# The gated delta rule's output, its projection and the norms: work by halves, fused ops by quarters

## The reference

```python
def layer_norm(x, g, b):
    mu = jnp.mean(x, -1, keepdims=True)
    var = jnp.mean(jnp.square(x - mu), -1, keepdims=True)
    return (x - mu) * lax.rsqrt(var + LN_EPS) * g + b

# the end of gdn_mixer
o = gated_delta_rule_chunked(q, k, v, g, beta)      # 4 chunks of 64 tokens, 8 heads of 128
o = o * lax.rsqrt(jnp.mean(o * o, -1, keepdims=True) + NORM_EPS) * norm_g
o = o * jax.nn.silu(z)
return o.reshape(bsz, seq, GDN_V) @ w_out
```

## Time and profile before

| what | us |
|---|---|
| median of 3 runs | 1741.26 |
| lowest and highest of the runs | 1740.02, 1744.06 |
| the profiled execution's own time | 1741.66 |
| its span in the profile | 1739.9 |
| PE busy | 1518.2 (87% of the span) |
| DVE busy | 1059.4 (61%) |
| ACT busy | 660.8 (38%) |
| mean DMA rate over the span | 254 GB/s read from HBM |

### The profile page before, as it was taken

The page is one execution under the profiler, slowest core; times in us unless marked ns, Lnnn a source line. Parts: engine busy times, 40 slices in busy tenths (PEclk is TensorE's granted clock), DMA queues, the critical chain, the costliest instruction groups (busy, mean ns, idle before and its releaser), DMA issues.

```text
span 1739.9 us, 23377 instructions
## 1 busy us (share of the span) xinstructions
PE 1518.2 (87%) x9936; PEld 1132.8 (65%) x9936; DVE 1059.4 (61%) x1522; ACT 660.8 (38%) x834; POOL 4.9 (0%) x6
## 2 busy tenths in 40 slices
PE   7987977999967678999999998598899999998976
PEld 7976846889956566888888886486444434443324
DVE  6646646999769857888989887765222221222145
ACT  5562104444421237676767774241211101110113
POOL 0010000000000000000000000000000000000000
PEclk9998988999978798999999999698899999999998
DMA  8440013453531054998989898166699999999970
GB/s 348 143 151 3 2 49 128 168 232 146 204 147 51 1 194 154 345 352 336 350 318 352 337 349 321 52 239 259 275 428 427 428 427 427 428 428 429 428 314 24
DMA packets 36685, 443.37 MB, mean 255 GB/s; under 512 B 5344, under 2 KB 5728, under 8 KB 9184
## 3 DMA queue, kind: packets, MB, share of 16 engines
q1 hardware_dynamic: 34992, 437.03, 63.1%
q10 hardware_dynamic: 1584, 4.77, 0.7%
HBM read 440.74 MB, written 1.05 MB: 254 GB/s over the span
## 4 chain that ended last, share of the span: by engine, by line
PE 52%; DVE 10%; DMA 8%; ACT 1%; issue 1%; DVEq 0%; PEld 0%; ACTq 0%; PEldq 0%
PE psum L223 50%; DMA sb_spare<-moe_up 2%; DMA sb_work<-moe_up 2%; DMA sb_ring<-moe_up 2%; DVE sb_work L1404 1%; DVE sb_work L1405 1%; DMA sb_ring<-moe_wide 1%; DVE sb_small L298 1%; DVE sb_work L2284 1%; DVE sb_split L1674 1%; PE psum L1727 1%; DMA sb_lnp<-pT 0%; PE psum L2154 0%; PE psum L339 0%; DVE sb_ring_r L268 0%
## 5 line engine op out<-in xcount | busy, mean ns | idle before, releaser
L223 PE MATMUL psum<-sb_work 64*64 64x64 f32 (+9 forms) x3056 | 304.7, 371 | 51.0 <-DVE sb_work L1389 13.9
L1674 DVE TENSOR_TENSOR sb_split<-sb_ring,sb_split 128x2048 fp32r<-128x2048 f32 (+1 forms) x144 | 301.1, 2111 | 45.3 <-ACT sb_split L1668 44.6
L1668 ACT ACTIVATE sb_split<-sb_ring 128x2048 fp32r<-128x2048 f32 (+1 forms) x144 | 253.0, 1773 | 88.7 <-PE psum L223 52.3
L223 PEld LDWEIGHTS psum<-sb_work 128*64 128x64 f32 (+4 forms) x3056 | 165.1, 155 | 177.5 <-issue 135.5
L223 PE MATMUL psum<-sb_split 128*128 128x512 f32 (+1 forms) x912 | 268.9, 384 | 0.3 <-DVE sb_split L1943 0.3
L223 PE MATMUL psum<-sb_split,sb_lnp_r 128*128 128x512 f32 (+1 forms) x768 | 230.8, 374 | 2.3 <-DVE sb_split L1912 1.4
L223 PEld LDWEIGHTS psum<-sb_split 128*128 128x128 f32 x912 | 169.9, 188 | 30.6 <-DVE sb_split L1943 1.1
L223 PEld LDWEIGHTS psum<-sb_split,sb_lnp_r 128*128 128x128 f32 x768 | 142.8, 188 | 22.9 <-DVE sb_split L1912 1.6
L223 PE MATMUL psum<-sb_ring,sb_work 128*64 128x512 f32 (+1 forms) x576 | 142.3, 598 | 8.5 <-DVE sb_work L2284 4.7
L223 PE MATMUL psum<-sb_xT_r,sb_ring_r 128*128 128x256 f32 x512 | 147.6, 288 | 0.0
L2282 DVE TENSOR_TENSOR sb_work<-sb_work,psum 128x512 f32<-128x512 f32 x16 | 11.0, 689 | 171.4 <-ACT sb_work L2198 171.4
(11 more groups left out here) (405 smaller groups left out, 2557.5 us busy)
## 6 DMA issues: line engine op xcount, KB each, us to landing
sb_ring<-moe_wide SPq DMA_DIRECT2D x48, 2048.0 KB, 9.0
sb_work<-moe_up SPq DMA_DIRECT2D x33, 2048.0 KB, 23.8
sb_ring<-w_dense SPq DMA_DIRECT2D x24, 2048.0 KB, 9.1
sb_ring<-moe_up SPq DMA_DIRECT2D x20, 2048.0 KB, 26.8
sb_work<-moe_down SPq DMA_DIRECT2D x20, 2048.0 KB, 27.0
sb_ring<-moe_last SPq DMA_DIRECT2D x24, 1536.0 KB, 8.2
sb_ring<-ffn_wide SPq DMA_DIRECT2D x12, 2048.0 KB, 7.8
sb_ring<-moe_down SPq DMA_DIRECT2D x12, 2048.0 KB, 27.6
```

Of the source, the lines that this page charges most:

```text
L223: return nc.tensor.matmul(o, lhsT, rhs, start=start, stop=stop, **kw)
L1668: act.activation(wh[half_home(e, i)][:, 0:half_size(i)], half_raw(e, i), ACT.Copy).then_inc(sem("m1_high"), 1)
L1674: v.tensor_tensor(wl[home][:, 0:half_size(i)], half_raw(e, i), wh[home][:, 0:half_size(i)].bitcast(F32), ALU.subtract).then_inc(sem("m1_sp ...
```

## The change

The diff below is cut to what the stages run; left out are the counts of semaphores in later stages.

- `norm_half` is new. For n < 4 a half is normed in two quarters of 512 columns by two fused ops each: `(x - mean) * g`, then `(. * rstd) + b`. The wait for g and b stands ahead of the first, the wait for the root between the two pairs. Each quarter counts in `rows_normed`. For n = 7 one fused op of 1024 columns does both products. For n = 4 to 6 the op stays. All `rows_normed` counts are doubled.
- PE turns a half by quarters for n < 4 (`turn_half`), each as soon as it is normed. For n = 0 the banks are 0 to 3 instead of 4 to 7.
- The end of the GDN mixer goes by halves. ACT takes over the square, in four ops of 128x512, and the root is taken once for each half. DVE's reduce, small ops and reciprocal of half 0 (`inverted(0)`) stand ahead of chunk 3's ops, its gating (`gated(0)`) ahead of chunk 3's sum.
- PE transposes half 0 of `o`, does its first product, transposes half 1, and does the products in the order (half 0, columns 0), (0, 1), (1, 0), the turn of the normed half 0, (1, 1). DVE norms half 0 behind its second product.
- `released` for `w_out` waits for the third and the fourth product instead of the second and the fourth.
- Some semaphores of later stages are shared by two events that come one after the other: `logitsT_ps` with `logits_ps`, `gates_ready` with `mask_ready`, and those of the two expert stages' row splits. No instruction other than the counts changes there.

```diff
@@ -306,56 +306,80 @@
             dve_link(v, v.tensor_scalar(rtmp[:, h, :], mv[:, h, 1:2], eps, None, ALU.add))
             v.reciprocal(rtmp[:, h, :], rtmp[:, h, :]).then_inc(sem("var_inv"), 1)
 
+        def norm_half(v, n, y, xn, h):
+
+            if n < 4:
+                quarters = (slice(0, 512), slice(512, 1024))
+                if h == 0:
+                    v.wait_ge(sem("lnp_loaded"), 32 * (n + 1))
+                for f in quarters:
+                    ins = v.scalar_tensor_tensor(xn[:, h, f], y[:, h, f], mv[:, h, 0:1], lnp[:, 0, f], ALU.subtract, ALU.mult)
+                dve_link(v, ins)
+                v.wait_ge(sem("rstd_ready"), 2 * n + h + 1)
+                for f in quarters:
+                    v.scalar_tensor_tensor(xn[:, h, f], xn[:, h, f], rstd[:, h, :], lnp[:, 1, f], ALU.mult, ALU.add)\
+                     .then_inc(sem("rows_normed"), 1)
+                return
+            v.wait_ge(sem("rstd_ready"), 2 * n + h + 1)
+            if n < 7:
+                v.tensor_scalar(xn[:, h, :], y[:, h, :], rstd[:, h, :], None, ALU.mult).then_inc(sem("rows_normed"), 2)
+            else:
+                v.scalar_tensor_tensor(xn[:, h, :], y[:, h, :], rstd[:, h, :], lnp[:, 0, :], ALU.mult, ALU.mult)\
+                 .then_inc(sem("rows_normed"), 2)
+
         def norm_vector(v, n, y, xn):
 
             for h in range(HALVES):
-                v.wait_ge(sem("rstd_ready"), 2 * n + h + 1)
-                if n < 4:
-                    dve_link(v, v.tensor_scalar(xn[:, h, :], y[:, h, :], mv[:, h, 0:1], rstd[:, h, :],
-                                                ALU.subtract, ALU.mult))
-                    if h == 0:
-                        v.wait_ge(sem("lnp_loaded"), 32 * (n + 1))
-                    dve_link(v, v.tensor_tensor(xn[:, h, :], xn[:, h, :], lnp[:, 0, :], ALU.mult))
-                    v.tensor_tensor(xn[:, h, :], xn[:, h, :], lnp[:, 1, :], ALU.add).then_inc(sem("rows_normed"), 1)
-                elif n < 7:
-                    v.tensor_scalar(xn[:, h, :], y[:, h, :], rstd[:, h, :], None, ALU.mult).then_inc(sem("rows_normed"), 1)
-                else:
-                    dve_link(v, v.tensor_scalar(xn[:, h, :], y[:, h, :], rstd[:, h, :], None, ALU.mult))
-                    v.tensor_tensor(xn[:, h, :], xn[:, h, :], lnp[:, 0, :], ALU.mult).then_inc(sem("rows_normed"), 1)
-            v.wait_ge(sem("rows_normed"), 2 * n + 2)
+                norm_half(v, n, y, xn, h)
+            v.wait_ge(sem("rows_normed"), 4 * n + 4)
 
         def norm_scalar(act, n):
             for h in range(HALVES):
-                act.wait_ge(sem("var_inv"), 2 * n + h + 1)
-                act.activation(rstd[:, h, :], rtmp[:, h, :], ACT.Sqrt).then_inc(sem("rstd_ready"), 1)
+                norm_root(act, n, h)
+
+        def norm_root(act, n, h):
+            act.wait_ge(sem("var_inv"), 2 * n + h + 1)
+            act.activation(rstd[:, h, :], rtmp[:, h, :], ACT.Sqrt).then_inc(sem("rstd_ready"), 1)
+
+        def turn_bank(n, h, q):
+            return bank[2 * h + q if n == 0 else 4 + 2 * h + q]
+
+        def turn_half(pe, n, xn, h):
+
+            for q in range(2):
...
 
             t = TSTAGE[n]
             for h in range(HALVES):
-                pe.wait_ge(sem("rows_normed"), 2 * n + h + 1)
-                for q in range(2):
-                    for c in range(4):
-                        ins = pe.transpose(bank[4 + 2 * h + q][:, c * P:(c + 1) * P],
-                                           xn[:, h, (4 * q + c) * P:(4 * q + c + 1) * P], ident)
-                    ins.then_inc(sem("turned"), 1)
+                if n > 0 or h > 0:
+                    turn_half(pe, n, xn, h)
             pe.wait_ge(sem("xT_ready"), 4 * (t + 1))
             if n in (0, 1):
                 pe.wait_ge(sem("xl_ready"), 4 * (n + 1))
 
         def turn_evacuate(eng, n, gain, dst=None):
 
+            for h in range(HALVES):
+                turn_half_evacuate(eng, n, gain, dst, h)
+
+        def turn_half_evacuate(eng, n, gain, dst, h):
+
             t = TSTAGE[n]
-            for h in range(HALVES):
-                for q in range(2):
-                    eng.wait_ge(sem("turned"), 4 * t + 2 * h + q + 1)
-                    o = (xT if dst is None else dst)[:, 4 * q:4 * q + 4, h * P:(h + 1) * P]
-                    i = bank[4 + 2 * h + q][:, :].rearrange("p (c t) -> p c t", c=4)
-                    if gain is None:
-                        ins = eng.activation(o, i, ACT.Copy)
-                    else:
-                        ins = eng.tensor_tensor(o, i, bc(gain[:, 4 * q:4 * q + 4], 2, P), ALU.mult)
-                    ins.then_inc(sem("xT_ready"), 1)
+            for q in range(2):
+                eng.wait_ge(sem("turned"), 4 * t + 2 * h + q + 1)
+                o = (xT if dst is None else dst)[:, 4 * q:4 * q + 4, h * P:(h + 1) * P]
+                i = turn_bank(n, h, q)[:, :].rearrange("p (c t) -> p c t", c=4)
+                if gain is None:
+                    ins = eng.activation(o, i, ACT.Copy)
+                else:
...
@@ -639,21 +663,27 @@
                                 ins = mm(bank3(6 + b)[rr, i, :], DTo[rr, j, :], vnew[rr, j, :])
                         ins.then_inc(sem("oi_ps"), 1)
 
-            for G in range(NGRP):
-                h, h0 = G // 2, HD * (G % 2)
+            def turned_out(h):
                 pe.wait_ge(sem("o_gated"), h + 1)
-                for i in range(HD):
-                    ins = pe.transpose(bank[G][:, i * P:(i + 1) * P], o_rows[:, HD * G + i, :], ident)
-                ins.then_inc(sem("ot_ps"), 1)
-
-            pe.wait_ge(sem("ot_done"), NGRP)
-            for j in range(2):
+                for G in (2 * h, 2 * h + 1):
+                    for i in range(HD):
+                        ins = pe.transpose(bank[G][:, i * P:(i + 1) * P], o_rows[:, HD * G + i, :], ident)
+                    ins.then_inc(sem("ot_ps"), 1)
+
+            def projected(h, j):
                 unit_ready(pe, U_WOUT + j)
+                pe.wait_ge(sem("ot_done"), 2 * h + 2)
                 w = slot(U_WOUT + j).rearrange("p (k n) -> p k n", k=DC)
-                for h in range(HALVES):
-                    for k in range(DC):
-                        ins = mm(bank[4 + 2 * j + h][:, :], oT[:, k, h * P:(h + 1) * P], w[:, k, :], k == 0, k == DC - 1)
-                    ins.then_inc(sem("wout_ps"), 1)
+                for k in range(DC):
+                    ins = mm(bank[4 + 2 * j + h][:, :], oT[:, k, h * P:(h + 1) * P], w[:, k, :], k == 0, k == DC - 1)
+                ins.then_inc(sem("wout_ps"), 1)
+            turned_out(0)
+            projected(0, 0)
+            turned_out(1)
+            projected(0, 1)
+            projected(1, 0)
+            turn_half(pe, 0, xres, 0)
+            projected(1, 1)
 
         def gdn_scalar(act):
             act.dma_start(conv_w, I["conv_w"]).then_inc(sem("first_loaded"), 16)
@@ -720,14 +750,27 @@
             for G in range(NGRP):
                 act.wait_ge(sem("wt_ps"), G + 1)
                 act.activation(grp(wT, G).rearrange("p i (c t) -> p c i t", c=2), wt_ps(G), ACT.Copy).then_inc(sem("wt_done"), 1)
-            act.wait_ge(sem("oms_inv"), 1)
-            act.activation(of[:, :, :], of[:, :, :], ACT.Sqrt).then_inc(sem("gates_act"), 1)
-            for G in range(NGRP):
-                h, h0 = G // 2, HD * (G % 2)
-                act.wait_ge(sem("ot_ps"), G + 1)
-                act.activation(oT[:, h0:h0 + HD, h * P:(h + 1) * P], bank3(G), ACT.Copy).then_inc(sem("ot_done"), 1)
-            norm_scalar(act, 0)
-            turn_evacuate(act, 0, None, xT_r)
+            def squared(h):
+                for G in (2 * h, 2 * h + 1):
+                    act.wait_ge(sem("o_sum"), G + 1)
+                    act.activation(grp(Wm, G), grp(o_rows, G), ACT.Square).then_inc(sem("o_squared"), 1)
+
+            def rooted(h):
+                act.wait_ge(sem("oms_inv"), h + 1)
+                act.activation(of[:, h, :], of[:, h, :], ACT.Sqrt).then_inc(sem("gates_act"), 1)
+            squared(0)
+            rooted(0)
+            squared(1)
+            for h in range(HALVES):
+                for G in (2 * h, 2 * h + 1):
+                    act.wait_ge(sem("ot_ps"), G + 1)
+                    act.activation(oT[:, HD * (G % 2):HD * (G % 2) + HD, h * P:(h + 1) * P], bank3(G), ACT.Copy)\
+                       .then_inc(sem("ot_done"), 1)
+                if h == 0:
+                    rooted(1)
+            for h in range(HALVES):
+                norm_root(act, 0, h)
+                turn_half_evacuate(act, 0, None, xT_r, h)
 
         def gdn_vector(v):
...
@@ -848,6 +891,25 @@
 
             v.wait_ge(sem("uu_done"), NGRP)
             v.wait_ge(sem("t_done"), 5 * NGRP)
+
+            def inverted(h):
+                v.wait_ge(sem("o_squared"), 2 * h + 2)
+                m, o, r = oms[:, h, :], of[:, h, :], rq_s[:, h, :]
+                dve_link(v, v.tensor_reduce(m, Wm[:, HEADS * h:HEADS * (h + 1), :], AX.X, ALU.add))
```

(46 more changed lines are left out.)

63 lines of the change are left out of this document (26 added, 37 removed).

## The result

The kernel with the change takes **1727.35 us** (median of four runs, 1726.48 to 1728.09) against 1741.9 for the kernel before in the same comparison (1740.02 to 1744.06): a ratio of 0.9917, 95% interval 0.9902 to 0.9932. Faster by 0.8%, inside the range of 1721 to 1731, and 1.95 us above the forecast of 1725.4. The profiled execution took 1727.54, its span is 1725.8 where it was 1739.9.

What follows compares the result with a forecast made beforehand. PE was taken to wait in short stretches while DVE works alone. Terms 5.8 + 4.5 + 1.1 + 2.0 + 1.35 + 1.5 = 16.25 us, off the profiled 1741.66, gave 1725.4; range 1721 to 1731.

Steps and rivals of the forecast that it cites:

- Bound and mechanism: Mixer's end: PE waits while DVE does one long serial string; move DVE work under PE work, shorten what is left.
- Part 1: Delta rule's end by halves: the first product starts at 227.4 instead of 235.39, 8.0 us earlier.
- Part 2: New order of the mixer's products: the last ends at 258.9 instead of 264.70, 5.8 us earlier.
- Part 3: Norm in two fused ops by quarters: 2.56 for a half, 4.5 us less after the mixer's last product.
- My nearest row from above: Price of the 512-wide fused op, taken from L1458, as wide with two sources: 0.69 us.
- Part 4: The other norms: 1.1 us after the FFN, 2.0 before the router, 1.35 ahead of the second block, 1.5 at the end.
- The clock: Mixer's first product: taken at the dear value after PE's pauses, 8.6 us against 6.9 at full clock.
- Rival A: Clock stays at 2.4 GHz over the pauses; the mixer's first product costs 6.9, 1.7 less: 1723.7; chance 0.33.
- Rival B: Gains shrink: fused ops without overlap, longer half-clock restarts in phases behind, DVE later than ScalarE needs: 1728 to 1733; chance 0.19.
- C: Clock stays at 1.2 GHz through all four mixer products as transposes break them up: 1751, slower; chance 0.02.
- D: Mixer's gain doesn't arrive: the FFN's first pieces wait for weights; 1738 to 1741; chance 0.02.
- What was put at nothing: Everything outside the touched stretches: forecast gain 0, later loads and phases only shifting with the phase ends.

Runs made afterwards that it cites:

- run 3: Changed kernel, but ScalarE copies the transposed half 0 before it takes the two squares of half 1; 1727.32 us, ratio 0.9913 to the kernel before.
- run 5: Changed kernel, but the two fused ops of norms 0 to 3 are 1024 wide instead of quarters; 1728.5 us, ratio 0.9925 to the kernel before.
- run 10: Changed kernel, but the first fused op of norms 0 and 2 subtracts the constant 0 instead of the mean; no whole time given.
- run 1: Changed kernel, but norms 0 to 3 are again the old three 1024-wide ops; 1732.63 us, ratio 0.9942 to the kernel before.
- run 8: Changed kernel with two useless DVE ops, 1.25 us each, just ahead of the first phase's end; 1729.92 us, ratio 0.9938 to the kernel before.
- run 9: The changed kernel once more, no edit; 1726.94 us, ratio 0.99 to the kernel before.
- run 12: Changed kernel with two useless 1024-wide DVE ops, a 2.5 us delay, ahead of the router's norm; 1730.37 us, ratio 0.9922 to the kernel before.
- run 6: Changed kernel, but both halves of norm 0, their turn and low parts come after all four products; 1727.13 us, ratio 0.9923 to the kernel before.
- run 4: Changed kernel with three useless matmuls in PE's pauses ahead of the first transposes and the first product; 1727.78 us, ratio 0.9915 to the kernel before.
- run 7: Changed kernel with run 3's edit and norm 1's rows of g and b loaded early in the FFN; 1725.42 us, ratio 0.9913 to the kernel before.
- run 11: Changed kernel with copies first, rows early, and the norm ahead of the second block 1024 wide; 1724.36 us, ratio 0.9878 to the kernel before.

## Why the prediction was right, and where it was off

**Bound and mechanism: right.** The time lay in stretches where PE waits for DVE, and 10.5 of some 14 us came from the mixer's end. A row of the chain by engine shows none of this; the idle times ahead of L646 and L339 did.

**Part 1, 8.0 us earlier: right.** Counted from the state update, the first product starts 8.0 earlier (20.18 before, 12.19 after), as summed; on the clock of the span it is 7.4 (228.00, and 227.4 forecast), since the whole stretch began 0.6 later in this execution. Its holder is ScalarE, squares ahead of copies, as told; run 3 shows that the other order is better by 1.1.

**Part 2, 5.8 us earlier: right.** The products end 5.5 earlier on the span's clock (259.16 for 264.70; 258.9 forecast), 6.1 counted from the state update. DVE was in time for half 0's turn: its norm ended at 249.4, 1.85 ahead of it, where 2.2 was forecast. The transposes of half 0 have no idle time before them.

**Part 3: the term that was mis-sized.** "0.69, starts 0.61 apart" was wrong. The fused op measures 0.75, starts 0.66 to 0.67 apart and 0.78 over the link, a half 2.78 (477.21 to 479.99) for my 2.56. (The expectation of run 5 has 0.71 apart, which no row shows.) Run 10 gives the cause: the scalar operand read from a tile adds 0.065 us to an op of this width. My nearest row from above, L1458, had no such operand; the earlier trace rows held a hint that I passed over, L314 with two tile scalars at 0.80 beside L323 with one at 0.75. Both sorts of op overlap with the one before (run 10: a pair with tile scalars 1.41, with constants 1.27). The Trainium skill's formula ("VectorE: DVE Perf Modes", section "The TRN2 errata — SBUF-src ops pay a fixed extra latency per instruction"), 0.691 for each op in full, made a half 2.76, by an estimate from that figure, and so came nearer than my row, but not by what the runs show as the cause: two ops with constants are not paid in full (1.27 for 1.38). At seven halves the 0.22 makes 1.5 us. The touched stretches missed by 0.45 only, as the mixer's end and the FFN's end gave 0.2 and 0.4 more than forecast; the tail at the mixer still gained 4.4 (14.62 to 10.24) for 4.5, since it holds one half only.

**Part 4.** Router 1.6 for 2.0 and second block 0.9 for 1.35: each short by two halves' 0.22. The end gave 1.3 for 1.5: its two ops took 1.24 each with the overlap where I had 1.23, so it is mostly the stretch from DVE's last op to the end, some 0.1 longer. FFN end 1.5 for 1.1, but one profile decides nothing here: the wait for the rows was 0 to 3.3 us over the runs that load them late.

**The clock.** Low in the first product, as in the sum: in after and in runs 1, 5, 8, 9 and 12 it took 8.8, in runs 6 and 10, with the same pauses ahead, 7.1. Rival A, to which I gave 0.33, is thus what some executions do. That the sum came out on the dear side is in part luck. Runs 3, 4, 7 and 11, with a pause shortened or filled, all ran at full clock (7.1); that the pauses are the cause rests on these four against six of eight. The Trainium skill ("TensorE: Matmul & The Clock Gate", section "Why this matters for your kernels") has only a longer pause throw the clock back; the two pauses here, 1.63 and 1.95 us with 1.09 us of transposes between, were enough in six of eight profiles, so by the measurement no single long pause is needed. Whether the transposes between the two count as work for the clock, or the two act as one pause, no run here tests.

**Rival B** was right in its first part, fused ops dearer than summed (not for want of overlap, but for their scalar), and in its second, restarts at half clock longer in the phases behind, at two places of the experts' stage (below). The result lies between its lower edge, 1728, and the forecast. C and D did not happen: the second and third products took 13.90 together at full clock, and the FFN's start moved by all that the mixer gained.

**What was put at nothing: all else.** It took 1.7 us longer in the profiled run, and that is the larger part of the 1.95 by which the forecast was under the time. Three stages make it up: the FFN 1.2 longer (198.85 to 200.09), the S5 stage 3.0 shorter (143.56 to 140.52), and the first block's experts, from the router's start to the third residual, 3.55 longer (427.08 to 430.63). The first two wander from one execution to the next (below). The third doesn't look like chance: the two profiles with the old norm ahead of the router (before and run 1) have 427.1 and 427.8, the twelve with the fused one 428.8 to 431.0. PE's rows show two places where the clock is low for longer. The router's first matmuls, before and after:

```profile
657.49 4.11 PE L223 MATMUL psum<-sb_xT,sb_router 128*8 128x128 f32 x32 [0.69 <-ACT sb_xT L355]
```
```profile
642.70 5.06 PE L223 MATMUL psum<-sb_xT,sb_router 128*8 128x128 f32 x32 [0.69 <-ACT sb_xT L379]
```
And the start of the stage's last matmuls, before and after, behind the same pause:
```profile
1078.74 0.73 PE L223 MATMUL psum<-sb_out_even,sb_selT_pair 128*128 128x512 f32 x2 [2.22 <-DVE sb_s_in_high L1920]
```
```profile
1065.61 1.22 PE L223 MATMUL psum<-sb_out_even,sb_selT_pair 128*128 128x512 f32 x2 [2.22 <-DVE sb_s_in_high L1972]
```
At the router the granted clock rose some 16 us after the last GLU products in both traces; the matmuls now start 1.6 earlier, so more of them run at 0.50, and 0.95 of the 1.6 goes back (the 32 matmuls take 4.3 in run 1 and 4.9 to 6.5 in the twelve). The sixteen last matmuls take 5.45 for 3.92, with the clock at 0.50 over their first 3 us where it was 1.00. That slow start is there in ten of the twelve profiles, but not in runs 4 and 5. Together the two places are 2.5 of the 3.55. From the last GLU products to the third residual the old norm has 441.7 and 442.5, the fused one 441.8 to 443.7 (run 12 left out): none of the 1.6 is seen there. Why the clock falls ahead of the last matmuls no run tests.

**What stays open.** Runs 8 and 12 show that a delay goes through to what follows. A gain need not: the one ahead of the router didn't arrive at the third residual. Besides, the untouched stages differ by up to 3.6 us from one execution to the next (FFN 198.4 to 202.0, the stage behind it 140.5 to 144.1). For the S5 stage this goes with the clock at its start: take one minus the granted clock, summed over its first 20 us. In seven profiles that is 1.4 to 2.1 us, and the stage takes 140.5 to 141.1; in the other seven it is 2.5 to 3.1, and the stage takes 142.9 to 144.1. So the shorter stretches of runs 3 and 4 could not be seen in their medians, nor the longer one of run 6. What sets the clock at a stage's start, and whether a stage that starts earlier meets it worse other than at the router, isn't settled.

## What to carry over

Where PE stands still, ask first what can go under PE work, then what is left to shorten: moving half 0's norm was worth 2.7 us at the mixer's end, fusing the ops 1.6 there. Follow a gain into the stage behind: of the 1.6 ahead of the router 0.95 went back at once, as the clock was still low when its matmuls began. Price a new op by a row with the same kinds of operands, not only the same width. In a short pause of PE look at which queue releases it, and at what that queue does first: two squares ahead of two copies cost 1.1 us, and mostly 1.7 more in a product that started at half clock.
